# Rounded matmuls that walk their columns and sums from the last to the first, in a two-layer hybrid trunk with experts

## The reference

```python
def swiglu(h, w_gate, w_up, w_down):
    return (jax.nn.silu(h @ w_gate) * (h @ w_up)) @ w_down

def moe_swiglu(h, w_router, w_gate, w_up, w_down):
    ...
    for e in range(N_EXPERTS):
        y = y + gates[:, e:e + 1].astype(t.dtype) * swiglu(t, w_gate[e], w_up[e], w_down[e])

def reference(x, g_mix, w_in, ...):
    for l in range(DEPTH):
        h = rms_norm(x, g_mix[l])
        qa, ka, va, qb, kb, vb, qc, kc, vc, qd, kd, vd, fd = _split_cols(h @ w_in[l])
        ...                                   # four attention groups
        x = x + jnp.concatenate(groups, axis=-1) @ w_out[l]
        h2 = rms_norm(x, g_ffn[l])
        x = x + (swiglu(h2, ...) if l % 2 == 0 else moe_swiglu(h2, ...))
    return x
```

## Time and profile before

| what | value |
|---|---|
| median of 3 runs | 1444.79 us (1444.56 to 1445.52) |
| the profiled execution | 1445.59 us, span 1443.7 us |
| TensorE busy | 1421.5 us (98%) |
| weight loads busy | 1150.3 us (80%) |
| VectorE busy | 1119.5 us (78%) |
| ScalarE busy | 935.8 us (65%) |
| DMA | 435.26 MB, mean 301 GB/s |
| granted TensorE clock | 1.00 all through |

### The profile page before, as it was taken

How to read it: one execution, slowest core, us unless ns; L and a number is a source line. 1 busy time by engine, 2 the same in 40 slices (tenths; PEclk the granted TensorE clock), 3 DMA queues, 4 the chain that set the end, 5 groups by cost and what they waited for, 6 DMA issues and landing times.

```text
span 1443.7 us, 16880 instructions
## 1 busy us (share of the span) xinstructions
PE 1421.5 (98%) x6622; PEld 1150.3 (80%) x6622; DVE 1119.5 (78%) x1277; ACT 935.8 (65%) x1234; POOL 82.5 (6%) x102
## 2 busy tenths in 40 slices
PE   7999999999999999999999999999999999999998
PEld 4885888886885778888888888888888888888886
DVE  3565455534566699989998998999999899898996
ACT  4544444424534588777777777777877777777773
POOL 2040000001031010000000000000000000000000
PEclk9999999999999999999999999999999999999999
DMA  9342565435142899999999999999999999999992
GB/s 354 112 143 106 205 234 196 153 136 199 59 151 82 325 394 389 379 385 391 367 379 388 369 378 392 371 373 389 374 372 385 388 364 376 394 379 362 398 377 90
DMA packets 180681, 435.26 MB, mean 301 GB/s; under 512 B 5557, under 2 KB 10357, under 8 KB 180469
## 3 DMA queue, kind: packets, MB, share of 16 engines
q1 hardware_dynamic: 177540, 423.11, 79.0%
q0 software_dynamic: 3056, 11.02, 1.9%
HBM read 428.33 MB, written 5.78 MB: 301 GB/s over the span
## 4 chain that ended last, share of the span: by engine, by line
PE 90%; DVE 4%; ACT 2%; POOL 1%; issue 1%; DMA 1%; SPq 0%; DVEq 0%; ACTq 0%
PE ps L1088 14%; PE ps L1090 14%; PE ps L1089 13%; PE ps L968 8%; PE ps L966 8%; PE ps L967 8%; PE ps L690 4%; PE ps L814 4%; PE ps L942 3%; PE ps L944 3%; PE ps L943 3%; DVE unit_rounded L1921 2%; PE ps L951 2%; PE ps L686 1%; PE ps L688 1%
## 5 line engine op out<-in xcount | busy, mean ns | idle before, releaser
L1921 DVE TENSOR_TENSOR unit_rounded<-wmem,unit_rounded 128x1024 fp32r<-128x1024 f32 (+1 forms) x744 | 854.1, 1210 | 77.5 <-ACT unit_rounded L1381 77.1
L1381 ACT ACTIVATE unit_rounded<-wmem 128x1024 fp32r<-128x1024 f32 (+1 forms) x744 | 719.7, 1043 | 119.8 <-PE ps L1090 59.6
L966 PE MATMUL ps<-unit_rounded,vbuf_rounded 128*128 128x512 f32 x528 | 205.7, 390 | 0.0
L968 PE MATMUL ps<-unit_rounded,stage_rounded 128*128 128x512 f32 x528 | 205.6, 389 | 0.0
L967 PE MATMUL ps<-unit_rounded,vbuf_rounded 128*128 128x512 f32 x528 | 205.4, 389 | 0.0
L1088 PE MATMUL ps<-unit_rounded,qkT_rounded 128*128 128x512 f32 x448 | 177.6, 396 | 0.8 <-DVE qkT_rounded L2084 0.8
L1088 PE MATMUL ps<-unit_rounded,hT_rounded 128*128 128x512 f32 x448 | 177.4, 396 | 0.0
L1090 PE MATMUL ps<-unit_rounded,qkT_rounded 128*128 128x512 f32 x448 | 174.8, 390 | 0.0
L1090 PE MATMUL ps<-unit_rounded,hT_rounded 128*128 128x512 f32 x448 | 174.8, 390 | 0.0
L1089 PE MATMUL ps<-unit_rounded,hT_rounded 128*128 128x512 f32 x448 | 174.5, 389 | 0.0
L1089 PE MATMUL ps<-unit_rounded,qkT_rounded 128*128 128x512 f32 x448 | 174.5, 389 | 0.0
(11 more groups left out here) (239 smaller groups left out, 1526.3 us busy)
## 6 DMA issues: line engine op xcount, KB each, us to landing
wmem<-in_w_exp_gate_dram SPq DMA_DIRECT2D x56, 2048.0 KB, 9.5
wmem<-in_w_exp_up_dram SPq DMA_DIRECT2D x56, 2048.0 KB, 10.0
wmem<-in_w_exp_down_dram SPq DMA_DIRECT2D x56, 2048.0 KB, 9.9
wmem<-in_w_in_dram SPq DMA_DIRECT2D x4, 3072.0 KB, 17.4
wmem<-in_w_ff_up_dram SPq DMA_DIRECT2D x5, 2048.0 KB, 8.9
wmem<-in_w_ff_gate_dram SPq DMA_DIRECT2D x5, 2048.0 KB, 9.1
wmem<-in_w_ff_down_dram SPq DMA_DIRECT2D x5, 2048.0 KB, 7.7
wmem<-in_w_out_dram SPq DMA_DIRECT2D x4, 2048.0 KB, 7.9
```

The costliest lines, as they stand in the source:

```text
L966: pe.matmul(o, hhb, hi[:, b, c], start=(first and b == 0), stop=False, skip_group_check=True)
L968: mm = pe.matmul(o, hlb, hi[:, b, c], start=False, stop=(b == blocks - 1), skip_group_check=True)
L1381: act.activation(quarter_r(HIGH[l][0 if last else kind], q, cols), quarter(SETS[l][i][kind], q, cols), ACT.Copy).then_inc(hi_ready[kind], 1)
L1921: dve.tensor_tensor(quarter_r(u, q, cols), quarter(u, q, cols), quarter_r(HIGH[l][0 if last else kind], q, cols), ALU.subtract).then_inc(l ...
```

## The change

A helper turns the last dimension of both the output and the moving operand: column 511 is streamed first and its sum written first, column 0 last. Each column still meets its own sum, so the values are the same. All fifteen calls that multiply rounded operands go through it; the plain ones stay.

```diff
+            def from_last(out, stationary, moving, start, stop, **kw):
+
+                return pe.matmul(out[:, ::-1], stationary, moving[:, ::-1], start=start, stop=stop, **kw)
...
-                    pe.matmul(o, xhk, hi[:, k, :], start=(k == 0), stop=False)
-                    pe.matmul(o, xhk, lo[:, k, :], start=False, stop=False)
-                    mm = pe.matmul(o, xlk, hi[:, k, :], start=False, stop=(k == KD - 1))
+                    from_last(o, xhk, hi[:, k, :], start=(k == 0), stop=False)
+                    from_last(o, xhk, lo[:, k, :], start=False, stop=False)
+                    mm = from_last(o, xlk, hi[:, k, :], start=False, stop=(k == KD - 1))
                 mm.then_inc((g_full, u_full)[kind], 2)
```

More of the change, by code:

```diff
@@ L685, in project @@
                             xh, xl = [part[l][:, k, t * P:(t + 1) * P] for part in (xs_high, xs_low)]
-                            pe.matmul(pbank(m)[:, 0:cols], xh, high_win[g][:, k, :], start=(k == 0), stop=False)
-                            pe.matmul(pbank(m)[:, 0:cols], xh, low_win[l][g][:, k, 0:cols], start=False, stop=False)
-                            mm = pe.matmul(pbank(m)[:, 0:cols], xl, high_win[g][:, k, :], start=False, stop=(k == KD - 1))
+                            from_last(pbank(m)[:, 0:cols], xh, high_win[g][:, k, :], start=(k == 0), stop=False)
+                            from_last(pbank(m)[:, 0:cols], xh, low_win[l][g][:, k, 0:cols], start=False, stop=False)
+                            mm = from_last(pbank(m)[:, 0:cols], xl, high_win[g][:, k, :], start=False, stop=(k == KD - 1))
                             continue
@@ L965, in down @@
                         o, c = ps[:, YB[t] + half, :], slice(half * 512, (half + 1) * 512)
-                        pe.matmul(o, hhb, hi[:, b, c], start=(first and b == 0), stop=False, skip_group_check=True)
-                        pe.matmul(o, hhb, lo[:, b, c], start=False, stop=False, skip_group_check=True)
-                        mm = pe.matmul(o, hlb, hi[:, b, c], start=False, stop=(b == blocks - 1), skip_group_check=True)
+                        from_last(o, hhb, hi[:, b, c], start=(first and b == 0), stop=False, skip_group_check=True)
+                        from_last(o, hhb, lo[:, b, c], start=False, stop=False, skip_group_check=True)
+                        mm = from_last(o, hlb, hi[:, b, c], start=False, stop=(b == blocks - 1), skip_group_check=True)
                 if not part_of or blocks - 1 in part_of:
@@ L1104, in last_down @@
                         o, c = ps[:, YB[0] + half, :], slice(half * 512, (half + 1) * 512)
-                        pe.matmul(o, hhb, hi[:, b, c], start=False, stop=False, skip_group_check=True)
-                        pe.matmul(o, hhb, lo[:, b, c], start=False, stop=False, skip_group_check=True)
-                        mm = pe.matmul(o, hlb, hi[:, b, c], start=False, stop=(b == 3), skip_group_check=True)
+                        from_last(o, hhb, hi[:, b, c], start=False, stop=False, skip_group_check=True)
+                        from_last(o, hhb, lo[:, b, c], start=False, stop=False, skip_group_check=True)
+                        mm = from_last(o, hlb, hi[:, b, c], start=False, stop=(b == 3), skip_group_check=True)
                     mm.then_inc(out_full, 1)
```

## The result

The changed kernel takes 1474.73 us (1473.4 to 1475.44, 4 runs) against 1444.82 us before (1444.56 to 1445.52, 4 runs): ratio 1.0205, interval 1.0188 to 1.0223. That is 29.9 us slower, 7 us beyond the top of the predicted range.

The account below looks back on a forecast made before the run. TensorE was taken as the bound, by the distance of rounded matmuls times their number. The profiled 1445.59 us plus 0 for all three costs, with the runs' median at 1444.79, gave 1445.0 us; range 1428 to 1468.

Parts of the forecast that it names:

- What bounds the kernel: TensorE, busy 934.79 of 936 us in the expert stage: rounded matmuls' start-to-start distance times their number, nearly all on the path.
- Step (a): In every rounded matmul, reading the moving operand from last column to first costs 0, since neighbours in time stay neighbours in memory.
- Step (b): In every rounded matmul, writing and accumulating the sums from last to first costs 0; trusted less than the reading.
- Step (c): The fixed 13.3 ns per rounded matmul, covering the switch from one to the next, changes by 0.
- half pace: Rival: each rounded matmul of 512 columns takes 0.430 us, total about 2480 us; chance 0.19 together with milder per-column losses.
- its milder form: Rival: a smaller per-column loss, such as a penalty only per line, anywhere between; within the 0.19 shared with half pace.
- The longer switch: Rival: only the fixed part per matmul grows, as one starting at a bank's far end needs a moment more; chance 0.08.
- a third more: Near case of the longer switch: 4.4 ns on each of 5160 matmuls, +23 us, 1468 us.
- the doubling: Far case of the longer switch: the fixed part per matmul doubled, +69 us, 1514 us.
- a switch effect: Sign in the trace: distances at 512 and 256 columns both shift by the same nanoseconds, independent of column count.
- The sign of being wrong: The distance between matmuls of 512 columns moves by over half a nanosecond (2.9 us over 5160 matmuls).

Follow-up runs that it names:

- the small kernel: A kernel of its own, nothing else running: sections of rounded matmuls of 128 x 128 by N columns; at 512 columns 226.7 ns rising, 233.3 ns falling.

## Why the prediction was wrong

- What bounds the kernel: right. TensorE's distance times the count gives the result to within half a microsecond, little of it was hidden, and no other engine became the limit. Beside it a drop of the clock cost about 1 us in the router, which the prediction did not have.
- Step (a), reading from last to first, cost 0: this is the step that failed. Measured: +6.7 ns settled, +6.0 ns in the mean, for each matmul of 512 columns, about 30 us in all (4972 x 6.0 = 29.8). My argument was that neighbours in time stay neighbours in memory. That is also true of rising reads from +8, which pay, and of fifteen in sixteen steps in blocks of 16 columns, which pay the full price. The argument looked at the moving stream alone; the runs show that for rising reads its place against the weight load matters too. Why the falling read pays stays open.
- Step (b), the sums, cost 0: right, although it was the one that I trusted less (ratio 0.9995). The strict reading of the Trainium skill (Advanced Engine Details and Errata, Memory Cachelines), by which any non-contiguous order in PSUM slows matmuls, does not hold for a step of -1. With the second sentence of that rule, by which every two consecutive elements should be contiguous, the trace agrees: 226.7 ns.
- Step (c), the fixed part: I split 226.7 ns into 213.3 and 13.3 from two widths and treated 13.3 as one switch. The widths of the small kernel show that this held for rising reads at 256, 320, 384 and 512 only (16.0 at 448, 58.4 at 128). For falling ones the same difference is 11.6, 13.3, 17.8, 20.0 and 20.0 from 256 to 512 columns, so it agrees at 320 alone.
- The rivals: half pace did not come (233, not 430 ns), nor its milder form, a price per column, which the widths exclude. The longer switch had the right sign and order of size, with a third more (4.4 ns, 1468 us) as its near case; the measured 6.0 ns lies between that and the doubling (1514). But its mechanism did not come either: it was a start at the far end of the bank, and blocks of 64 begin in the tile's last 64 columns and cost nothing. So its nearness in size is luck. It had 0.08, and my range ended at its near case. A third was a choice and no reading; the doubling would have been the bound to take.
- The signs that I named: a switch effect was to shift both widths by the same nanoseconds. They shifted by +6.7 and -1.5, which fits none of the patterns that I named. The sign of being wrong, more than half a nanosecond at 512 columns, was met, and running the two walks one at a time was the test that decided.
- A small misreading: the profiled execution, 1445.59 us, lies 0.07 above the scatter that I said it was within. Nothing hangs on it.

## What to carry to other kernels

Where TensorE is the bound, write down the start-to-start distance of its main form and compare it with its column count: 13 ns of 227 here are not columns, and they move with how operands lie. For rounded (fp32r) matmuls of 512 columns, start moving tile and stationary block at a multiple of 256 bytes, or at least at the same place modulo 256 bytes and on a multiple of 32 bytes (a common shift of 4 bytes cost 237.9 ns). Read rising, or in blocks of at least 256 bytes if the order has to be turned. The sums may be written from last to first for nothing. An argument that an operand's order costs nothing should be checked against both reads that TensorE makes, the moving one and the weight load, and its range should reach to the full size of what is left unexplained.

## What the runs showed of the hardware

- Start addresses are worth up to 5% on rounded matmuls of 512 columns: 226.7 ns with both reads at a multiple of 256 bytes, 238.6 ns with the moving one 4 bytes on. bf16 with the moving read at +8 columns (16 bytes there) stays at 216 ns, the only moved start that was tried in bf16.
- Falling inside blocks of 16 bytes or less is free (2 or 4 columns, 226.7 ns). Falling inside blocks of 64 bytes is the dearest order seen that skips no column (266.7 ns). Every second column costs 451 ns, every fourth 461 ns. The Trainium skill (Advanced Engine Details and Errata, Memory Cachelines) asks for at least two hits on each 16-byte line of SBUF; every second column has two, and the trace does not agree that this is enough here.
- A stationary block with fewer columns loads faster (188 ns with 128 columns, 109 with 32), but the matmuls of 512 columns do not follow each other faster (226.7 and 231.6 ns), nor do they with 64 rows (226.7).
- At 256 columns the order turns round: 120.0 ns with both reads at a multiple of 256 bytes, 116.7 ns with the moving one 8 columns on, 118.3 with the stationary one so. This kernel has 96 such matmuls, 0.3 us, under what can be measured.

Open is what the two reads share, and why a falling read pays the same wherever the stationary block lies. At 512 columns, no order or start that was tried beats the kernel before.
